# The gate/up projection of the second layer's feed-forward as seven block products, with one of four weight sums on GpSimd

## The chip, the cores and the metric

The kernel runs on one core of one Trainium2 chip. The time is the device time of one execution, in microseconds (us); the kernel before was run three times.

## The reference

Two layers of a diffusion backbone, 512 latent tokens and 256 context tokens of width 1024, all in 32-bit floating point. Each layer is a mixer (gating and attention), then a gated feed-forward; norms and modulation surround both. The second layer works on the latent tokens alone. The change is in its feed-forward:

```python
def conv_ffn(h, w_in, conv_w, conv_b, w_out):
    z = h @ w_in
    g = dwconv(z[..., :D_FF], conv_w, conv_b)
    return (jax.nn.silu(g) * z[..., D_FF:]) @ w_out
```

with D_FF = 2816, so that `w_in` is 1024 x 5632. The convolution is over three neighbouring tokens, feature by feature.

## The kernel before, in words

Every large product is made of three matmuls. A 32-bit factor is split into a high part (rounded to the matmul's format) and a low part (the rest): high x high, high x low and low x high are added in PSUM (`split_mm`, lines 293, 297 and 301). Weights come in slots of 128 x 2048 numbers (1 MB): SyncE loads slot n into `w_raw[n % 2]` (`w_load`, line 341) once VectorE has finished with slot n - 2; ScalarE rounds it (`round_hi`, line 276); VectorE subtracts (`take_lo`, line 282).

The feed-forward of the second layer (stage "ff1") has 22 slots. A slot holds 128 gate features and the 128 up features that belong to them, for all eight 128-row pieces of the depth 1024. `feature_slot` runs 48 matmuls on it (2 feature groups, 8 pieces of depth, 3 matmuls), each over 512 tokens, into two PSUM banks. The first two slots are special (`first_slots`): the tokens come out of the norm in two groups of 256, so there the matmuls are over 256 tokens, interleaved with the transposes of the second group. The other 20 slots are loops.

What follows a slot: ScalarE applies the middle tap of the convolution to the gate bank (`yb`, line 945), VectorE adds the two outer taps (line 988, twice, with a drain between), ScalarE applies SiLU (line 955), VectorE multiplies with the up bank into `A_ff_lat` (line 1001) and signals `evac`. Each engine has its own queue and takes its instructions strictly in the written order; engines wait for each other by semaphores. In `ffn_act` and `ffn_dve` these steps stand beside the rounding of the next slot, in two buffers each. The output product (stage "ffo1", `out_pe`, lines 608, 611 and 614) follows; its left factors are split by `part_hi` (line 676) and `part_lo` (line 682), the first three of them already in the last slot.

Ahead of the stage, `out_then_norm_...` ends the mixer: VectorE scales the norm (line 456), TensorE transposes (line 519), VectorE and ScalarE scale and shift into six small buffers `pre_tmp`, ScalarE rounds, VectorE and GpSimd (line 487) each make half of the low parts in `HT`.

## Time and profile before

| | us |
|---|---|
| median of 3 runs | 1748.36 |
| lowest and highest run | 1747.74, 1748.41 |
| span of the profiled execution, first to last instruction | 1744.6 |
| run median less that span (what lies around it) | 3.8 |
| TensorE busy | 1699.8 |
| VectorE busy | 1102.7 |
| ScalarE busy | 683.5 |
| GpSimd busy | 195.1 |

The profile is of one execution. The page gives the span alone; the time of the runs lies 3.8 us above it. A matmul's time in the profile is longer than the distance to the next one, since matmuls overlap: what a row of matmuls costs is read from the distance between starts.

### The profile page before, as it was taken

How to read it: one execution, taken by the hardware profiler on the slowest of the kernel's cores; microseconds unless marked ns; L12 is line 12 of the kernel's file. 1: busy time of each engine (PE TensorE's matmuls, PEld its weight loads, DVE VectorE, ACT ScalarE, POOL GpSimd, SP SyncE). 2: the span in 40 equal slices, each digit the busy share in tenths (PEclk: the TensorE clock that was granted, in tenths of full speed). 3: DMA queues.
4: the chain of work that ended last, by engine and by line, in shares of the span. 5: the costliest groups of instructions: out<-in, count | busy, mean ns of one | idle time of the engine just before them, and what ended most of it. 6: DMA issues, size and time to landing. Idle time of an engine off the chain costs nothing.

```text
span 1744.6 us, 23609 instructions
## 1 busy us (share of the span) xinstructions
PE 1699.8 (97%) x9234; PEld 1454.8 (83%) x9234; DVE 1102.7 (63%) x1745; ACT 683.5 (39%) x1127; POOL 195.1 (11%) x201
## 2 busy tenths in 40 slices
PE   6999999999999999999999999999999999999998
PEld 4788899787988888888888898879887888888777
DVE  5676777767676766644344678978875644444454
ACT  4343266544422221223344444454455422223442
POOL 1078500002100000000000210111210200000000
PEclk9999999999999999999999999999999999999999
DMA  8633000131334345441312122200012222222321
GB/s 343 215 124 116 17 22 1 75 143 49 133 128 162 138 152 193 169 134 55 114 50 95 40 102 80 97 1 1 33 42 86 95 73 96 97 97 97 131 98 71
DMA packets 40769, 173.08 MB, mean 99 GB/s; under 512 B 12640, under 2 KB 13152, under 8 KB 26208
## 3 DMA queue, kind: packets, MB, share of 16 engines
q1 hardware_dynamic: 31984, 166.75, 26.5%
q10 hardware_dynamic: 8688, 4.99, 1.0%
q8 instruction: 66, 1.08, 0.3%
q14 instruction: 31, 0.25, 0.1%
HBM read 169.60 MB, written 2.13 MB: 98 GB/s over the span
## 4 chain that ended last, share of the span: by engine, by line
PE 87%; DVE 4%; ACT 3%; DVEq 2%; issue 1%; DMA 1%; POOL 1%; ACTq 0%; SPq 0%; another core or an unknown queue 0%
PE PS L297 14%; PE PS L293 14%; PE PS L301 14%; PE PS L608 8%; PE PS L614 8%; PE PS L611 8%; PE PS L1120 4%; PE PS L325 3%; PE PS L328 3%; PE PS L329 3%; PE PS L1105 2%; DMA mod_raw<-modw 1%; DVE w_lo L282 1%; DVEq L1165 1%; ACT w_hi L276 1%
## 5 line engine op out<-in xcount | busy, mean ns | idle before, releaser
L293 PE MATMUL PS<-HT,w_hi 128*128 128x512 f32 (+1 forms) x1248 | 375.6, 347 | 0.0
L297 PE MATMUL PS<-HT,w_hi 128*128 128x512 f32 (+1 forms) x1248 | 375.5, 347 | 0.0
L301 PE MATMUL PS<-HT,w_lo 128*128 128x512 f32 (+1 forms) x1248 | 372.1, 344 | 0.0
L282 DVE TENSOR_TENSOR w_lo<-w_raw,w_hi 128x2048 fp32r<-128x2048 f32 x100 | 231.4, 2314 | 168.4 <-ACT w_hi L276 162.3
L608 PE MATMUL PS<-w_hi,a_ring 128*128 128x512 f32 x670 | 262.8, 392 | 2.9 <-DVE w_lo L282 0.9
L611 PE MATMUL PS<-w_lo,a_ring 128*128 128x512 f32 x670 | 260.9, 389 | 0.0
L276 ACT ACTIVATE w_hi<-w_raw 128x2048 fp32r<-128x2048 f32 x99 | 188.9, 1908 | 160.9 <-PE PS L608 103.7
L301 PEld LDWEIGHTS PS<-HT,w_lo 128*128 128x128 f32 x1248 | 211.7, 189 | 31.9
L293 PEld LDWEIGHTS PS<-HT,w_hi 128*128 128x128 f32 x1248 | 209.5, 188 | 29.9
L297 PEld LDWEIGHTS PS<-HT,w_hi 128*128 128x128 f32 x1248 | 210.6, 189 | 28.5
L988 DVE SCALAR_TENSOR_TENSOR yb<-PS,cws,yb 128x511 f32<-128x511 f32 (+1 forms) x132 | 83.1, 658 | 155.4 <-ACTq L949 151.0
L945 ACT ACTIVATE yb<-PS,cws 128x512 f32<-128x512 f32 x44 | 34.3, 780 | 338.4 <-PE PS L301 338.4
L608 PEld LDWEIGHTS PS<-w_hi,a_ring 128*128 128x128 f32 x670 | 125.8, 188 | 32.7 <-DVE w_lo L282 3.0
L611 PEld LDWEIGHTS PS<-w_lo,a_ring 128*128 128x128 f32 x670 | 125.8, 188 | 25.3
L819 POOL TENSOR_TENSOR rstd<-rstd,halfneg 128x1 f32<-128x1 f32 x20 | 11.0, 550 | 1145.1 <-DVE rstd L771 1145.0
L614 PE MATMUL PS<-w_hi,a_ring 128*128 128x512 f32 x340 | 132.4, 389 | 0.0
L415 DVE SCALAR_TENSOR_TENSOR m_raw<-m_raw,c_rows 128x1024 f32<-128x1024 f32 x80 | 102.1, 1276 | 30.9 <-DMA m_raw<-modu 28.9
L325 PE MATMUL PS<-w_hi,HT 128*128 128x512 f32 (+1 forms) x272 | 103.1, 379 | 0.5 <-DVE HT L1964 0.5
L329 PE MATMUL PS<-w_hi,HT 128*128 128x512 f32 (+1 forms) x272 | 102.0, 375 | 0.0
L328 PE MATMUL PS<-w_lo,HT 128*128 128x512 f32 (+1 forms) x272 | 102.0, 375 | 0.0
L2096 DVE SCALAR_TENSOR_TENSOR cat_od<-G,ccw,cat_od 128x512 f32<-128x512 f32 x120 | 86.0, 751 | 4.3 <-issue 0.4
L1164 DVE TENSOR_REDUCE rmax<-PS 128x1 f32<-128x768 f32 (+1 forms) x72 | 66.6, 924 | 15.9 <-PE PS L1082 14.4
(321 smaller groups left out, 2660.0 us busy)
## 6 DMA issues: line engine op xcount, KB each, us to landing
w_raw<-wpack SPq DMA_DIRECT2D x102, 1024.0 KB, 4.8
m_raw<-modu SPq DMA_DIRECT2D x80, 512.0 KB, 4.3
mod_raw<-modw SPq DMA_DIRECT2D x8, 1024.0 KB, 11.7
c_rows<-c_scratch SPq DMA_DIRECT2D x6, 512.0 KB, 5.2
X<-x SPq DMA_DIRECT2D x2, 1024.0 KB, 6.5
out<-X SPq DMA_DIRECT2D x4, 512.0 KB, 2.6
X<-ctx SPq DMA_DIRECT2D x1, 1024.0 KB, 10.0
gmB<-gate_rows_evo ACTq DMA_DIRECT2D x1, 1024.0 KB, 4.5
```

What stands on the lines that cost most here:

```text
L276: nc.scalar.activation(w_hi[r][:, :], w_raw[r][:, :], ACT.Copy).then_inc(wh_ready, 1)
L282: nc.vector.tensor_tensor(w_lo[r][:, :], w_raw[r][:, :], w_hi[r][:, :].bitcast(F32), ALU.subtract).then_inc(wl_ready, 1)
L293: mm = nc.tensor.matmul(o, wh, xh, start=start, stop=False)
L297: mm = nc.tensor.matmul(o, wh, xl, start=False, stop=False)
L301: last = nc.tensor.matmul(o, wl, xh, start=False, stop=stop)
L325: mm = nc.tensor.matmul(o, xh, w_hi[r][:, wc], start=k == 0, stop=False)
L328: nc.tensor.matmul(o, xh, w_lo[r][:, wc], start=False, stop=False)
L329: return nc.tensor.matmul(o, xl, w_hi[r][:, wc], start=False, stop=k == KD - 1)
L415: nc.vector.scalar_tensor_tensor(out=raw if g == sets - 1 else ps2(m_banks(c)[0], D), in0=raw, scalar=1.0, in1=c_rows[c_phase(c)][g][:, :] ...
L608: mm = nc.tensor.matmul(o, ah, w_hi[n % 2][:, wc], start=k == 0, stop=False)
L611: mm = nc.tensor.matmul(o, ah, w_lo[n % 2][:, wc], start=False, stop=False)
L614: return nc.tensor.matmul(o, al, w_hi[n % 2][:, wc], start=False, stop=k == kt - 1)
```

## The change

In slots 2 to 21 of "ff1" the product is written as a 2 x 2 block product. The blocks are: gate or up features; even or odd pieces of the depth; first or second 128 tokens of each group of 256. The eight block products become seven. Each is 12 matmuls over 256 tokens, so a slot has 84 in place of 48 of 512. Four of the seven use sums or differences of weight blocks (`Sw`), the others plain blocks; four use differences of token blocks (`TH`, `TL`, made once). All seven weights are split into `FH[0..6]` (ScalarE, `form_hi`, seven roundings of 512 numbers) and `FL[0..6]` (VectorE, `form_lo`). Three of the sums are made by VectorE (`form_sum` 0, 1, 3), one by GpSimd (`third_sum`). Products share three PSUM banks x, w, y; several are added onto a bank whose content is first copied out by ScalarE (`seven_keep`: p1, p5, u2, u3). VectorE joins the parts: `gate` makes `Gf`, from which the convolution now reads; `up_sum` adds the two kept pieces in `zp`; `evacuate` multiplies in two halves. The loops are written out. The norm ahead keeps its values in `h_pre3` and no longer in the six buffers; GpSimd and VectorE make the token differences there. Some semaphores are shared under other names. The order of the loads on SyncE is as before; a load's release is now the seventh `form_lo` of the slot two before.

```diff
+        h_pre3 = [at("h_pre3_0", R_X + 16 * KIB, [P, KD, 256]), at("h_pre3_1", R_A + 8 * KIB, [P, KD, 256])]
+        TH, TL = ([at(f"{name}{i}", off + part * 4 * KIB, [P, KD // 2, 2, P], F32R) for i, off in
+                   enumerate((R_HT + 32 * KIB, R_HT + 40 * KIB, R_A + 44 * KIB, R_A + 52 * KIB))]
+                  for part, name in enumerate(("TH", "TL")))
+        FH, FL = ([at(f"{name}{i}", off + (i % 4) * 2 * KIB + (1 - i // 4) * 8 * KIB, [P, KD // 2, P], F32R) for i in range(7)]
+                  for off, name in ((R_WH, "FH"), (R_WL, "FL")))
+        Sw = [at(f"Sw{i}", R_MOD + 2 * i * KIB, [P, KD // 2, P]) for i in range(4)]
+        pu = at("pu", R_A + 60 * KIB, [P, 2, 256])
+        zp = at("zp", R_A + 62 * KIB, [P, 2, 256])
+        up = at("up", R_A + 64 * KIB, [P, LAT])
+        Gf = at("Gf", R_GM + 6 * KIB, [P, LAT])
 
...
+        SUM_OF = {1: 0, 2: 1, 4: 2, 5: 3}
+        RAW_OF = {0: (0, 0), 3: (1, 0), 6: (1, 1)}
+        RIGHT_OF = {0: (0, 0), 3: (1, 0), 5: (1, 1)}
+        TURNED_OF = {1: 0, 2: 1, 4: 2, 6: 3}
+        BANK_OF = ("x", "y", "x", "w", "x", "y", "x")
+        ONTO = (2, 4, 5, 6)
+        TURNED = (0, 2, 1, 3)
...
+        def formed(s, i):
+            return 6 * s + ((0, 2, 3, 1, 4, 5)[i] if s == 0 else i) + 1
...
+        def product_done(eng, s, i):
+            if i == 6:
+                eng.wait_ge(w_used, F11 + 2 + s + 1)
+            else:
+                eng.wait_ge(S("sv", "prod"), 6 * s + i + 1)
+        def form_sum(dve, s, j):
+            n = F11 + 2 + s
+            a11, a12, a21, a22 = (raw_part(n, k, m) for m in range(2) for k in range(2))
+            if j == 0:
+                raw_landed(dve, n)
+            if j == 3:
+                dve.wait_ge(S("sv", "sum"), 3 * s + 2)
+            x, y, op = {0: (a21, a22, ALU.add), 1: (Sw[0][:, :, :], a11, ALU.subtract),
+                        3: (a12, Sw[1][:, :, :], ALU.subtract)}[j]
+            nc.vector.tensor_tensor(Sw[j][:, :, :], x, y, op).then_inc(S("sv", "sum"), 1)
+        def third_sum(pool, s):
+            n = F11 + 2 + s
+            raw_landed(pool, n)
+            if s:
+                pool.wait_ge(S("sv", "lo"), formed(s - 1, 4))
+            nc.gpsimd.tensor_tensor(Sw[2][:, :, :], raw_part(n, 0, 0), raw_part(n, 0, 1), ALU.subtract)\
+                .then_inc(S("sv", "tsum0"), 1)
+        def form_hi(act, s, i):
+            if i == 4:
+                act.wait_ge(S("sv", "tsum0"), len(TURNED) + s + 1)
+            elif i in SUM_OF:
+                act.wait_ge(S("sv", "sum"), 3 * s + {1: 1, 2: 2, 5: 3}[i])
+            else:
+                raw_landed(act, F11 + 2 + s)
+            if s:
+                product_done(act, s - 1, i)
+            else:
+                act.wait_ge(w_used, F11 - 1 if i < 4 else F11 + 2)
+            nc.scalar.activation(FH[i][:, :, :], form_source(s, i), ACT.Copy)\
+                .then_inc(wh_ready if i == 6 else S("sv", "hi"), 1)
+        def form_lo(dve, s, i):
+            if i == 6:
+                dve.wait_ge(wh_ready, F11 + 2 + s + 1)
+            else:
+                dve.wait_ge(S("sv", "hi"), formed(s, i))
+            nc.vector.tensor_tensor(FL[i][:, :, :], form_source(s, i), FH[i][:, :, :].bitcast(F32), ALU.subtract)\
+                .then_inc(wl_ready if i == 6 else S("sv", "lo"), 1)
...
+        def turned_sum(eng, ops, g, t):
+            if t == 0:
+                eng.wait_ge(S("pre3", "hi"), since("pre3", "hi") + KD * (g + 1))
+                eng.wait_ge(S("pre3", "lo_even"), since("pre3", "lo_even") + KD // 2 * (g + 1))
+            if t == 1:
+                eng.wait_ge(S("pre3", "lo_odd"), since("pre3", "lo_odd") + KD // 2 * (g + 1))
+            eng.drain()
+            b11, b12, b21, b22 = (half_tokens(g, k, h) for k in range(2) for h in range(2))
+            x, y = ((b12, b11), (b22, b11), (b22, b12), (b21, b22))[t]
+            ops.tensor_tensor(turned_place(g, t), x, y, ALU.subtract).then_inc(S("sv", f"tsum{g}"), 1)
...
+        def seven_pe(pe):
+            first_slots(pe, "pre3", F11, 2)
+            for s in range(JF - 2):
+                ns = s + 2
+                for i in range(7):
+                    if i == 6:
+                        pe.wait_ge(wl_ready, F11 + ns + 1)
+                    else:
+                        pe.wait_ge(S("sv", "lo"), formed(s, i))
+                    if i == 0:
+                        pe.wait_ge(S("ff1", "evac"), since("ff1", "evac") + s + 1)
+                    if s == 0 and i in TURNED_OF:
+                        pe.wait_ge(S("sv", "tlo"), 2 * TURNED.index(TURNED_OF[i]) + 2)
+                    if i in (2, 4, 5, 6):
+                        pe.wait_ge(S("sv", "kept"), 4 * s + {2: 1, 4: 3, 5: 3, 6: 4}[i])
+                    o = PS[:, seven_bank(ns, BANK_OF[i]), 0:256].rearrange("p (g c) -> p g c", g=2)
+                    for q in range(KD // 2):
+                        if i in RIGHT_OF:
+                            k, h = RIGHT_OF[i]
+                            xh, xl = (HT[:, 0:2, part, 2 * q + k, h * P:(h + 1) * P] for part in range(2))
+                        else:
+                            t = TURNED_OF[i]
+                            xh, xl = TH[t][:, q, :, :], TL[t][:, q, :, :]
+                        onto = i in ONTO
+                        begins, ends = q == 0 and not onto, q == KD // 2 - 1
+                        nc.tensor.matmul(o, FH[i][:, q, :], xh, start=begins, stop=False, skip_group_check=onto)
+                        nc.tensor.matmul(o, FH[i][:, q, :], xl, start=False, stop=False, skip_group_check=onto)
+                        last = nc.tensor.matmul(o, FL[i][:, q, :], xh, start=False, stop=ends, skip_group_check=onto)
+                    last.then_inc(w_used if i == 6 else S("sv", "prod"), 1)
...
+        def seven_keep(act, s, which):
+            ns = s + 2
+            what, i, dst = {"p1": ("x", 0, pu[:, 0, :]), "p5": ("y", 1, zp[:, 1, :]), "u2": ("x", 2, pu[:, 1, :]),
+                            "u3": ("x", 4, zp[:, 0, :])}[which]
+            product_done(act, s, i)
+            if s and which == "p1":
+                act.wait_ge(S("sv", "gate"), s)
+            if s and which == "p5":
+                act.wait_ge(S("sv", "up"), s)
+            nc.scalar.activation(dst, PS[:, seven_bank(ns, what), 0:256], ACT.Copy).then_inc(S("sv", "kept"), 1)
...
+            for g in range(2):
+                turned_hi(act, g, 0)
+            plain(0)
+            form_hi(act, 0, 1)
+            for g in range(2):
+                turned_hi(act, g, 2)
+            silu(0)
+            form_hi(act, 0, 2)
+            for t in (1, 3):
+                for g in range(2):
+                    turned_hi(act, g, t)
+            plain(1)
+            form_hi(act, 0, 4)
+            form_hi(act, 0, 5)
+            silu(1)
+            form_hi(act, 0, 6)
+            for s in range(JF - 2):
+                ns, last = s + 2, s == JF - 3
+                def next_hi(i):
+                    if not last:
+                        form_hi(act, s + 1, i)
+                seven_keep(act, s, "p1")
+                next_hi(0)
+                seven_keep(act, s, "p5")
+                if s:
+                    silu(ns - 1)
+                next_hi(1)
+                seven_keep(act, s, "u2")
+                next_hi(2)
+                if last:
+                    act.wait_ge(S("ff1", "evac"), since("ff1", "evac") + JF - 1)
+                    part(0)
+                    part(1)
+                    product_done(act, s, 3)
+                    round_hi(act, F21)
+                next_hi(3)
+                seven_keep(act, s, "u3")
+                next_hi(4)
+                act.wait_ge(S("sv", "gate"), s + 1)
+                act.wait_ge(S("ff1", "evac"), since("ff1", "evac") + ns - 1)
+                conv_tap(ns, Gf[:, :])
+                next_hi(5)
+                next_hi(6)
+            silu(JF - 1)
+            act.wait_ge(w_used, F21)
+            part(2)
+            round_hi(act, F21 + 1)
...
+            def gate(s):
+                dve.wait_ge(S("sv", "kept"), 4 * s + 3)
+                product_done(dve, s, 5)
+                w = seven_bank(s + 2, "w")
+                nc.vector.tensor_tensor(by_half(Gf[:, :]), pairs(PS[:, w:w + 2, 0:256]), pairs(pu[:, :, :]), ALU.add)\
+                    .then_inc(S("sv", "gate"), 1)
+            def up_sum(s):
+                dve.wait_ge(S("sv", "kept"), 4 * s + 4)
+                nc.vector.tensor_tensor(up[:, 0:256], zp[:, 0, :], zp[:, 1, :], ALU.add).then_inc(S("sv", "up"), 1)
+            def evacuate(s):
+                j = s + 2
+                dve.wait_ge(S("ff1", "silu"), since("ff1", "silu") + j + 1)
+                dve.wait_ge(S("sv", "up"), s + 1)
+                product_done(dve, s, 6)
+                y, a = by_half(yb[j % 2][:, 0:LAT]), by_half(A_ff_lat[:, j, :])
+                x = PS[:, seven_bank(j, "x"), 0:256].rearrange("p (g c) -> p g c", g=2)
+                nc.vector.tensor_tensor(a[:, 0], y[:, 0], x, ALU.mult)
+                nc.vector.tensor_tensor(a[:, 1], y[:, 1], up[:, 0:256].rearrange("p (g c) -> p g c", g=2), ALU.mult)\
+                    .then_inc(S("ff1", "evac"), 1)
+            for t in TURNED:
+                turned_sum(dve, nc.vector, 1, t)
+            form_lo(dve, 0, 0)
+            form_lo(dve, 0, 3)
+            form_sum(dve, 0, 0)
+            for g in range(2):
+                turned_lo(dve, g, 0)
+            conv(0, PS[:, 0, :])
+            form_sum(dve, 0, 1)
+            form_sum(dve, 0, 3)
+            form_lo(dve, 0, 1)
+            for g in range(2):
+                turned_lo(dve, g, 2)
+            gated(0, PS[:, 1, :])
+            form_lo(dve, 0, 2)
+            for t in (1, 3):
+                for g in range(2):
+                    turned_lo(dve, g, t)
+            conv(1, PS[:, 3, :])
+            form_lo(dve, 0, 4)
+            form_lo(dve, 0, 5)
+            gated(1, PS[:, 4, :])
+            form_sum(dve, 1, 0)
+            for s in range(JF - 2):
+                ns, last = s + 2, s == JF - 3
+                def next_lo(i):
+                    if not last:
+                        form_lo(dve, s + 1, i)
+                def next_sum(j):
+                    if not last:
+                        form_sum(dve, s + 1, j)
+                form_lo(dve, s, 6)
+                if s:
+                    conv(ns - 1, Gf, lambda: next_sum(0))
+                else:
+                    dve.drain()
+                next_sum(1)
+                next_lo(0)
+                if s:
+                    up_sum(s - 1)
+                next_lo(1)
+                if s:
+                    evacuate(s - 1)
+                next_sum(3)
+                next_lo(2)
+                if last:
+                    part(0)
+                next_lo(3)
+                next_lo(4)
+                if last:
+                    take_lo(dve, F21)
+                gate(s)
+                next_lo(5)
+            conv(JF - 1, Gf)
+            part(1)
+            up_sum(JF - 3)
+            evacuate(JF - 3)
+            part(2)
+            take_lo(dve, F21 + 1)
...
+        def seven_pool(pool):
+            for t in (1, 3):
+                turned_sum(pool, nc.gpsimd, 0, t)
+            for s in range(JF - 2):
+                third_sum(pool, s)
...
                 round_hi(act, n_next + 1)
+                form_hi(act, 0, 0)
+                form_hi(act, 0, 3)
                 pre_high(act, sp, KD, 2 * KD)
...
             else:
+                for t in (0, 2):
+                    turned_sum(pool, nc.gpsimd, 0, t)
                 pre_low(pool, sp, KD, 2 * KD)
...
-            ffn_act(act, "ff1", 1, F11, LAT, lambda q: part_hi(act, "ffo1", q, JF, LT, A_ff_lat))
+            seven_act(act, lambda q: part_hi(act, "ffo1", q, JF, LT, A_ff_lat))
...
-            ffn_pe(pe, "ff1", F11, LAT, False, "pre3")
+            seven_pe(pe)
...
-            ffn_dve(dve, "ff1", 1, F11, LAT, A_ff_lat, False, lambda q: part_lo(dve, "ffo1", q, JF, LT, A_ff_lat))
+            seven_dve(dve, lambda q: part_lo(dve, "ffo1", q, JF, LT, A_ff_lat))
```

**VectorE, the end of one slot of the loop before and the next slot.** `w_raw` is the loaded slot, `cws` the taps, `yb` the gate branch, `PS` PSUM:

```order
L1001 TENSOR_TENSOR A_ff_lat<-yb_170,PS 128x512
L281 REGISTER_ALU
L282 TENSOR_TENSOR w_lo_56<-w_raw_52,w_hi_54 128x2048 [waits wh_ready]
L973 ISA
L973 COPY cws_89<-cw 128x4
L983 REGISTER_ALU
L988 SCALAR_TENSOR_TENSOR yb_171<-PS,cws_89,yb_171 128x511 [waits ff1_mid]
L988 SCALAR_TENSOR_TENSOR yb_171<-PS,cws_89,yb_171 128x511
```

**VectorE, from `gate` of one slot into the next slot, in the change.** L828 is `gate`, L661 `form_lo`, L629 `form_sum`, L807 and L811 the two outer taps, L833 `up_sum`, L842 and L843 `evacuate`; `ff_mid` comes from ScalarE's middle tap, `sv_hi` from its roundings, `sv_kept` from its copies:

```order
L828 TENSOR_TENSOR Gf<-PS,pu 128x2x2x128 [waits sv_prod,sv_kept]
L661 TENSOR_TENSOR FL_211<-Sw_216,FH_204 128x512 [waits sv_hi]
L661 TENSOR_TENSOR FL_212<-w_raw_52,FH_205 128x512 [waits wh_ready]
L807 SCALAR_TENSOR_TENSOR yb_165<-Gf,cw,yb_165 128x511 [waits ff_mid]
L629 TENSOR_TENSOR Sw_213<-w_raw_51 128x512 [waits landed0]
L811 SCALAR_TENSOR_TENSOR yb_165<-Gf,cw,yb_165 128x511
L629 TENSOR_TENSOR Sw_214<-Sw_213,w_raw_51 128x512
L661 TENSOR_TENSOR FL_206<-w_raw_51,FH_199 128x512 [waits sv_hi]
L833 TENSOR_TENSOR up<-zp 128x256 [waits sv_kept]
L661 TENSOR_TENSOR FL_207<-Sw_213,FH_200 128x512 [waits sv_hi]
L842 TENSOR_TENSOR A_ff_lat<-yb_165,PS 128x2x128 [waits w_used,sv_up,ff_silu]
L843 TENSOR_TENSOR A_ff_lat<-yb_165,up 128x2x128
```

The five instructions of a slot became sixteen (twelve are shown); the taps stand behind `gate` and two `form_lo`, `evacuate` behind `up_sum` and a `form_lo`.

**ScalarE, two slots before** (L276 rounds the next slot, L945 is the middle tap, L955 SiLU):

```order
L276 ACTIVATE w_hi_54<-w_raw_52 128x2048 [waits w_used,landed1]
L945 ACTIVATE yb_171<-PS,cws_89 128x512 [waits w_used,ff1_tap]
L955 ACTIVATE yb_171<-yb_171 128x512 [waits ff1_conv]
L276 ACTIVATE w_hi_53<-w_raw_51 128x2048 [waits w_used,landed0]
L945 ACTIVATE yb_170<-PS,cws_88 128x512 [waits w_used,ff1_tap]
L955 ACTIVATE yb_170<-yb_170 128x512 [waits ff1_conv]
```

**ScalarE, from the middle tap of one slot to the third copy of the next, in the change.** L743 is the middle tap, L652 `form_hi`, L738 `seven_keep`, L748 SiLU:

```order
L743 ACTIVATE yb_164<-Gf,cw 128x512 [waits ff_evac,sv_gate]
L652 ACTIVATE FH_204<-Sw_216 128x512 [waits sv_prod,sv_sum]
L652 ACTIVATE FH_205<-w_raw_51 128x512 [waits w_used,landed0]
L738 ACTIVATE pu<-PS 128x256 [waits sv_gate,sv_prod]
L652 ACTIVATE FH_199<-w_raw_52 128x512 [waits sv_prod,landed1]
L738 ACTIVATE zp<-PS 128x256 [waits sv_up,sv_prod]
L748 ACTIVATE yb_164<-yb_164 128x512 [waits ff_conv]
L652 ACTIVATE FH_200<-Sw_213 128x512 [waits sv_prod,sv_sum]
L738 ACTIVATE pu<-PS 128x256 [waits sv_prod]
L652 ACTIVATE FH_201<-Sw_214 128x512 [waits sv_prod,sv_sum]
L652 ACTIVATE FH_202<-w_raw_52 128x512 [waits sv_prod,landed1]
```

Here the second copy of the slot (`zp`) waits for `sv_up`, VectorE's `up_sum`; SiLU, the rounding of `FH_200` and the copy after it stand behind that wait.

## Rows read from the trace of the kernel before

**Rows 1.** The page, busy time of each engine (us, share of the span, instructions).
```profile
PE 1699.8 (97%) x9234; PEld 1454.8 (83%) x9234; DVE 1102.7 (63%) x1745; ACT 683.5 (39%) x1127; POOL 195.1 (11%) x201
```
**Rows 2.** Stretches: length, busy us of PE, PEld, DVE, ACT, POOL, granted clock, DMA share, GB/s.
```profile
1398.40:1615.80 217.40, 217.40 (x960) 180.06 (x960) 91.86 (x101) 65.54 (x62) 0.00 (x0) 1.00 0.26 95
...
20.00:40.00 20.00, 17.27 (x97) 10.89 (x96) 11.55 (x21) 7.90 (x9) 0.00 (x0) 0.91 1.00 394
...
1374.00:1384.00 10.00, 7.08 (x59) 6.67 (x59) 8.27 (x16) 5.58 (x9) 3.06 (x5) 1.00 0.27 102
```
**Rows 3.** Timeline of TensorE: start us, us, instruction, count [idle before it <- releaser].
```profile
1374.56 0.28 PE L297 MATMUL PS<-HT,w_next_hi 128*128 128x256 f32 x1
1374.68 0.28 PE L301 MATMUL PS<-HT,w_next_lo 128*128 128x256 f32 x1
1377.50 0.44 PE L519 MATMUL PS<-ident,xn_pre 128*128 128x128 f32 x2 [2.54 <-DVE xn_pre L456]
...
1398.23 0.40 PE L293 MATMUL PS<-HT,w_hi 128*128 128x512 f32 x1
...
1439.74 0.39 PE L293 MATMUL PS<-HT,w_hi 128*128 128x512 f32 x1
1439.96 0.39 PE L297 MATMUL PS<-HT,w_hi 128*128 128x512 f32 x1
...
1615.86 0.39 PE L608 MATMUL PS<-w_hi,a_ring 128*128 128x512 f32 x1
...
1621.76 0.50 PE L608 MATMUL PS<-w_hi,a_ring 128*128 128x512 f32 x1 [0.30 <-DVE w_lo L282]
```
**Rows 4.** Timeline of ScalarE and VectorE in a slot of the loop.
```profile
1444.42 0.63 ACT L955 ACTIVATE yb<-yb 128x512 f32<-128x512 f32 x1 [1.66 <-DVE yb L988]
1444.96 1.90 ACT L276 ACTIVATE w_hi<-w_raw 128x2048 fp32r<-128x2048 f32 x1
...
1442.81 1.57 DVE L988 SCALAR_TENSOR_TENSOR yb<-PS,cws,yb 128x511 f32<-128x511 f32 x2 [4.43 <-ACTq L949]
1446.89 2.29 DVE L282 TENSOR_TENSOR w_lo<-w_raw,w_hi 128x2048 fp32r<-128x2048 f32 x1 [1.00 <-ACT w_hi L276]
```
**Rows 5.** VectorE's groups (count | busy us, mean ns | idle before), and three instructions in a row.
```profile
L682 DVE TENSOR_TENSOR A_ff_lat_lo<-A_ff_lat,a_ring 128x512 fp32r<-128x512 f32 x22 | 13.8, 685 | 0.1
L475 DVE TENSOR_TENSOR HT<-pre_tmp_pre,HT 128x256 fp32r<-128x256 f32 x32 | 13.7, 427 | 1.3 <-ACT HT L508 0.6
...
1627.08 1.89 DVE L682 TENSOR_TENSOR a_ring<-A_ff_lat,a_ring 128x512 fp32r<-128x512 f32 x3
```
**Rows 6.** ScalarE's groups, and two of its instructions in a row.
```profile
L676 ACT ACTIVATE a_ring<-A_ff_lat 128x512 fp32r<-128x512 f32 x43 | 25.1, 620 | 22.3 <-PE PS L614 17.2 <-DVE A_ff_lat L1001 2.5 <-DVE cws L973 2.4
L1043 ACT ACTIVATE qTh<-PS 128x256 fp32r<-128x256 f32 x8 | 3.1, 384 | 1.0 <-PE PS L1030 0.7
...
1313.98 1.51 ACT L1627 ACTIVATE cat_od<-cat_od,ccln 128x512 f32<-128x512 f32 x2
```
**Rows 7.** Timeline of ScalarE and VectorE ahead of the loop.
```profile
1392.73 0.78 ACT L945 ACTIVATE yb<-PS,cws 128x512 f32<-128x512 f32 x1 [5.70 <-PE PS L301]
...
1393.57 1.57 DVE L988 SCALAR_TENSOR_TENSOR yb<-PS,cws,yb 128x511 f32<-128x511 f32 x2 [4.13 <-ACTq L949]
1395.84 0.69 DVE L1001 TENSOR_TENSOR A_ff_lat<-yb,PS 128x512 f32<-128x512 f32 x1 [0.70 <-ACT yb L955]
```
**Rows 8.** GpSimd beside VectorE: a group of GpSimd, then three instructions of the timeline.
```profile
L1403 POOL TENSOR_TENSOR sqs<-sqs,sqs 128x512 f32<-128x512 f32 x3 | 4.0, 1326 | 0.5 <-issue 0.5
...
1368.93 1.28 DVE L813 SCALAR_TENSOR_TENSOR X<-O_both_odo,rstd,X 128x1024 f32<-128x1024 f32 x1
1370.49 0.60 DVE L475 TENSOR_TENSOR HT<-pre_tmp_pre,HT 128x256 fp32r<-128x256 f32 x1 [0.29 <-ACT HT L508]
...
1369.59 1.22 POOL L487 TENSOR_TENSOR HT<-pre_tmp_pre,HT 128x256 fp32r<-128x256 f32 x1 [1.30 <-ACT HT L508]
```
**Rows 9.** The page, DMA issues: KB each, median us from issue to landing.
```profile
w_raw<-wpack SPq DMA_DIRECT2D x102, 1024.0 KB, 4.8
```

109 lines of the change are left out of this document (81 added, 28 removed).

## The prediction

> **What bounds the kernel now.** I read the page first, then the second feed-forward by stretches and in order of time. TensorE is busy for 97% of the span, the others for far less [rows 1]. In the 217.4 us of slots 2 to 21 it never pauses: 217.4 us busy, at full granted clock, VectorE 91.9, ScalarE 65.5, GpSimd nothing [rows 2]. The loop starts at 1398.23 and the output product at 1615.86, so a slot takes 217.63 / 20 = 10.88 us. That is 48 starts 0.22 to 0.23 us apart; where matmuls run over 256 tokens, starts are 0.12 apart [rows 3]. VectorE and ScalarE wait in every slot, since one short chain follows it and nothing waits for that chain at once [rows 4]. So TensorE's own work is the bound, and fewer columns would shorten the stage, as long as the work fed to TensorE keeps up.
>
> **What TensorE gains.** Seven products of 12 matmuls at 0.12 us are 84 x 0.12 = 10.08 us a slot, 0.80 less than now, or 16 us over 20 slots. I take 0.12 for any weights, since only the shape sets it in those rows.
>
> **What a slot now asks of VectorE and ScalarE.** Prices first. A VectorE `tensor_tensor` of 512 numbers lasts 0.685 us, but three in a row last 1.89, so the next starts after 0.60; one of 256 lasts 0.43 and, with the same 0.09 taken off, frees the engine after 0.34, with 0.35 used here [rows 5]. Two taps with a drain between last 1.57, one alone 0.75; so a drain adds 0.07, and a tap frees the engine after 0.66 [rows 4, 5]. ScalarE: 512 numbers 0.62, free after 0.54 (SiLU start to the next start); 256 from PSUM 0.384, free after 0.30; 512 from SBUF with scale and bias 0.80, free after 0.71 (1.51 less 0.80) [rows 4, 6]. From the end on one engine to the start on another pass 0.03 to 0.04: rounding ends at 1446.86 and VectorE starts at 1446.89, the taps end at 1444.38 and SiLU starts at 1444.42 [rows 4]. I take 0.035.
>
> Busy time alone fits: VectorE 11 x 0.60 + 1.50 + 0.35 + 0.70 = 9.15 us, ScalarE 7 x 0.54 + 4 x 0.30 + 0.71 + 0.54 = 6.2, both under 10.08. But each queue is in written order and the two wait for each other twice in a slot. Starting at `gate` and ending at the next slot's `gate`, the ring is:
> - `gate` 0.685 + 0.035 to ScalarE: 0.72.
> - Middle tap 0.71, then the rounding of piece 5 0.62 + 0.035: 1.365. VectorE has only `form_lo` 5 next, so it stands still.
> - `form_lo` 5 and 6: 1.20.
> - First outer tap 0.66, the sum put between (0.685 and 0.07 for the drain, 0.76), second tap 0.66: 2.08.
> - `form_sum` 1 and `form_lo` 0: 1.20.
> - `up_sum` 0.43 + 0.035: 0.465. ScalarE has waited for it with the copy "p5", because `zp` holds the last slot's part.
> - That copy 0.30, SiLU 0.54, the rounding of piece 1 0.62 + 0.035: 1.495. VectorE stands still again, at `form_lo` 1.
> - `form_lo` 1 0.60, `evacuate` 2 x 0.35, `form_sum` 3 and `form_lo` 2, 3, 4 2.40: 3.70.
>
> Together 12.22 us. Nothing in it depends on TensorE: that needs the copy "u2" before product 4, which comes 0.3 us behind the rounding of piece 1, and then it pauses about 2.1 us a slot. So **the ring, not TensorE, sets the slot**: 12.22 against 10.88, 1.34 us worse.
>
> **The ends.** Ahead of the loop TensorE now waits for `evac` of slot 0. VectorE starts the taps of slot 0 at about 1393.6 as now [rows 7]; then come 1.50, five `tensor_tensor` (3.0) and the multiplication (0.69), end 1398.8: 0.6 after the loop's old start. In the first seven-product slot, ScalarE's first copy stands behind SiLU of slot 1, which waits for VectorE: six `tensor_tensor` after 1398.1 (3.6), taps 1.57, then SiLU, a rounding and the copy, end about 1404.8; product 2 wants it at 1398.85 + 2.88 = 1401.7. That slot ends at about 1412.1, 13.9 after 1398.23, so 3.0 worse than now. Then 18 slots at +1.34 are 24.1, and the last, where the next slot's steps fall away and one whole weight slot is split, takes some 11.3 (+0.4). The output product starts 27.5 later. There its third part waits for `gate`, tap (0.72 + 0.84), taps 1.57, SiLU 0.54, part 0.54, rounding 1.9 and subtraction 2.29, about 8.5 us after 1643.3, thus at 1651.8, against 1621.76 now, a shift of 30.0 [rows 3]. Later parts keep it.
>
> **Edits that I cost at nothing.** The load of a slot is issued after `form_lo` 6, lands 4.8 us later [rows 9], and is first read in the following slot, some 8 us later; a later release would eat that first. In the norm the six small buffers fall away, and their waits with them; TensorE there waits for the scaled norm, which stays [rows 3]. The two roundings in front (1.1 us) fit in the 2.8 us in which ScalarE waits for scaled values. GpSimd's two token sums there (1.27 us each [rows 8]) may keep VectorE from the subtraction that TensorE waits for behind the pause at 1377.50: 0 to 1.0 us, taken as 0.
>
> **GpSimd's weight sum.** A sum of 512 numbers takes GpSimd 1.27 us, or up to 1.43 (the mean of three is 1.33) [rows 8]. It starts when `form_lo` 4 ends, beside `gate` (which reads PSUM) and VectorE's wait of 1.4 us, and its result is wanted most of a slot later. So it costs nothing, and saves VectorE 0.60 on the ring, already left out above. What it could cost: GpSimd and VectorE hinder each other. A GpSimd instruction of 256 numbers that usually takes 0.74 took 1.22 beside one of VectorE with two SBUF inputs, and the VectorE instruction behind it took 0.60 in place of 0.43 [rows 8]. The bound is 0 to 1.3 us a slot; I take 0. The Trainium skill (SBUF — State Buffer, Who interferes with whom) says that a GpSimd instruction reading SBUF and a VectorE one with two SBUF inputs exclude each other altogether, whoever comes first. By that rule, and if the sum fell on the ring, each slot would lose up to GpSimd's whole 1.3 us; the rows show the exclusion and smaller losses. That is a rival below.
>
> The Trainium skill (VectorE: DVE Perf Modes, The DRAIN you can't avoid) also says that the next VectorE operation doesn't start until the pipe is empty, though one that isn't held may start earlier. If all eleven on the ring went at 0.685 the slot would be 13.2 us; the rows above show 0.60 in a row.
>
> **Sum.** 1748.4 + 30.0 = 1778.4 us (span 1744.6 + 30 = 1774.6; what lies around it, 3.8, stays).
>
> **The rivals.**
> - **The products win** (faster). If VectorE and ScalarE stay a slot ahead, TensorE sets the pace from slot 3 on: 13.9 + 19 x 10.08 = 205.4 against 217.6, and with the 2.4 at the output product 1738.5 us. For it: both are under 10.08 us busy. Against: the ring closes within a slot and gets no shorter by starting early. It decides once the ring is under 10.88; the whole wait at `form_lo` 1 and some of that at `form_lo` 5 would have to go. 0.04.
> - **Only the first of the two stops counts**: were the copy "p5" not in ScalarE's way, VectorE's ring would be 12.22 less 1.96 (`up_sum`, copy, SiLU, rounding) plus 0.35, 10.6 us, and the time about 1748.5, no change. Against: in the order above ScalarE's rows stand as counted. 0.06.
> - **GpSimd or the drain lies on the ring too**: 1.0 to 1.3 us more a slot, 1797 to 1803. Speaks for it: rows 8; against: the sum's place beside `gate`. 0.07.
> - **The change doesn't do what it says**: TensorE's work doesn't shrink, because the pauses cost it its clock. A granted clock of 0.91 stands early in the program, between 20 and 40 us, where TensorE had long idled; around the single pause of 2.54 us it is 1.00 [rows 2, 3]. At the lower of the two levels (1.2 in place of 2.4 GHz) a matmul of 256 would last about 0.23, as one of 512 does now, 84 x 0.23 = 19.3 us a slot: 1748 + 170. 0.03.
>
> **How the numbers follow.** My forecast has 0.80. Its own spread: with no time between engines and 0.57 for 0.60 the ring is 11.8 and the time 1770; with 0.64, and copies that free ScalarE only after 0.42, it is 12.8 and 1790. The range 1766 to 1792 holds it nearly whole and leaves the rivals out. Around 0.2% (3.5 us) is what can be told from no change: slower 0.90, same 0.05, faster 0.05.
>
> **What would show it.** In the profile after, TensorE's first matmuls of a slot lie 12.2 us apart, with a pause of about 2 us before product 4 put down to ScalarE's copy; `form_lo` 1 and `form_lo` 5 wait 1.3 to 1.6 us each for ScalarE's rounding; "p5" waits for `up_sum`; GpSimd's sum takes 1.3 us. Slots 10.1 apart without pauses would prove me wrong, as would `form_lo` 1 that never waits.

## The result, and the profile after

Four runs of the changed kernel have a median of 1805.74 us (1803.64 to 1807.28), four of the kernel before beside them 1748.05 (1746.98 to 1748.41). The ratio is 1.0331, 95% interval 1.0317 to 1.0346. The forecast was 1778.4, range 1766 to 1792: the sign was right, the slow-down twice what was said. The span grew from 1744.6 to 1804.6 us, by 60.0; the sum had 30.0.

The page after, busy time of each engine, against [rows 1]:

```profile
PE 1718.2 (95%) x9954; PEld 1507.1 (84%) x9954; DVE 1210.3 (67%) x1975; ACT 751.9 (42%) x1335; POOL 230.3 (13%) x225
```

TensorE's busy time rose from 1699.8 to 1718.2 us, though each slot has 84 short matmuls where it had 48 long ones and should need less. The stretches say why (columns as in [rows 2]): the granted clock is no longer 1.00.

```profile
1430.00:1460.00 30.00, 26.25 (x193) 25.90 (x192) 20.26 (x35) 15.22 (x31) 2.59 (x3) 0.89 0.21 70
1460.00:1660.00 200.00, 171.86 (x1221) 169.25 (x1220) 138.00 (x236) 92.62 (x190) 18.13 (x14) 0.87 0.23 80
1660.00:1700.00 40.00, 36.90 (x208) 31.58 (x208) 24.14 (x30) 19.61 (x27) 0.00 (x0) 1.00 0.36 122
```

TensorE's timeline in one slot, where [rows 3] had starts 0.12 apart throughout:

```profile
1451.72 0.36 PE L723 MATMUL PS<-TH,FH 128*128 128x256 f32 x1 [1.88 <-ACT pu L738]
...
1452.16 0.41 PE L723 MATMUL PS<-TH,FH 128*128 128x256 f32 x1
1452.38 0.41 PE L724 MATMUL PS<-TL,FH 128*128 128x256 f32 x1
...
1455.15 0.41 PE L725 MATMUL PS<-HT,FL 128*128 128x256 f32 x1
1455.37 0.36 PE L723 MATMUL PS<-HT,FH 128*128 128x256 f32 x1
1455.56 0.28 PE L724 MATMUL PS<-HT,FH 128*128 128x256 f32 x1
```

Ahead of product 4 TensorE pauses 1.88 us for ScalarE's copy "u2" (`pu`, L738), as foreseen. Then, from the fourth matmul on, 15 lie (1455.37 - 1452.16) / 15 = 0.214 us apart, and after that 0.12 again. Three short stretches of this slot, before, in and behind that piece:

```profile
1442.80:1451.60 8.80, 7.05 (x59) 6.84 (x58) 5.76 (x10) 4.48 (x10) 0.90 (x1) 1.00 0.36 121
1452.10:1455.30 3.20, 3.20 (x17) 3.20 (x17) 2.44 (x6) 1.42 (x3) 0.00 (x0) 0.50 0.00 0
1455.40:1463.00 7.60, 7.60 (x65) 7.60 (x65) 5.63 (x9) 2.76 (x5) 1.29 (x1) 0.99 0.26 77
```

For 3.2 us the granted clock is 0.50, the lower of the two levels (1.2 GHz), and 1.00 up to the pause. The Trainium skill (TensorE: Matmul & The Clock Gate, Part 1: The HAM clock gate) says that at that level matmuls start their columns divided by 1.2 GHz apart. For 256 columns that makes an estimate of 0.213 us, and the trace agrees with its 0.214. From the start of product 4 to that of product 6, at 1456.16, pass 4.44 us, where 24 starts at 0.12 would be 2.88: 1.5 us too many.

VectorE and ScalarE in that slot:

```profile
1442.76 0.69 DVE L828 TENSOR_TENSOR Gf<-PS,pu 128x512 f32<-128x512 f32 x1 [0.50 <-PE PS L725]
1444.85 0.69 DVE L661 TENSOR_TENSOR FL<-Sw,FH 128x512 fp32r<-128x512 f32 x1 [1.41 <-ACT FH L652]
...
1449.38 0.42 DVE L833 TENSOR_TENSOR up<-zp 128x256 f32<-128x256 f32 x1
1451.34 0.69 DVE L661 TENSOR_TENSOR FL<-Sw,FH 128x512 fp32r<-128x512 f32 x1 [1.54 <-ACT FH L652]
...
1455.26 0.69 DVE L661 TENSOR_TENSOR FL<-Sw,FH 128x512 fp32r<-128x512 f32 x1 [0.76 <-ACT FH L652]
1456.43 0.69 DVE L828 TENSOR_TENSOR Gf<-PS,pu 128x512 f32<-128x512 f32 x1 [0.48 <-PE PS L725]
```

```profile
1449.89 0.38 ACT L738 ACTIVATE zp<-PS 128x256 f32<-128x256 f32 x1 [3.42 <-PE PS L725]
1450.17 0.62 ACT L748 ACTIVATE yb<-yb 128x512 f32<-128x512 f32 x1
1450.69 0.62 ACT L652 ACTIVATE FH<-Sw 128x512 fp32r<-128x512 f32 x1
1451.20 0.37 ACT L738 ACTIVATE pu<-PS 128x256 f32<-128x256 f32 x1
```

`form_lo` 5 waits 1.41 us and `form_lo` 1 waits 1.54, as foreseen (1.3 to 1.6). The copy "p5" (`zp`) is put down to TensorE, but that was long done: it starts 0.09 us after `up_sum` (L833) ends. What is new are the waits of 0.76 us at `form_lo` 4 and 0.48 at `gate`, for product 5. The slot is 1456.43 - 1442.76 = 13.67 us, and the 18 from gate to gate are 246.5 us in all, 13.70 each.

### The profile page after: what moved, and what is told of

Read it like the earlier page. It is cut to its first block and busy times, and to the rows that moved or that the text cites. A ratio compares the mean times of both kernels' runs of the same rounds, so it can differ in the third digit from the quotient of the medians.

```text
span 1804.6 us, 25614 instructions
## 1 busy us (share of the span) xinstructions
PE 1718.2 (95%) x9954; PEld 1507.1 (84%) x9954; DVE 1210.3 (67%) x1975; ACT 751.9 (42%) x1335; POOL 230.3 (13%) x225
## 5 line engine op out<-in xcount | busy, mean ns | idle before, releaser
L297 DVE TENSOR_TENSOR w_lo<-w_raw,w_hi 128x2048 fp32r<-128x2048 f32 x80 | 186.1, 2326 | 149.3 <-ACT w_hi L291 145.0
L308 PE MATMUL PS<-HT,w_hi 128*128 128x256 f32 (+1 forms) x928 | 251.1, 332 | 0.0
L312 PE MATMUL PS<-HT,w_hi 128*128 128x256 f32 (+1 forms) x928 | 251.0, 332 | 0.0
L316 PE MATMUL PS<-HT,w_lo 128*128 128x256 f32 (+1 forms) x928 | 247.6, 328 | 0.0
L291 ACT ACTIVATE w_hi<-w_raw 128x2048 fp32r<-128x2048 f32 x80 | 152.8, 1910 | 163.1 <-PE PS L958 106.1
L316 PEld LDWEIGHTS PS<-HT,w_lo 128*128 128x128 f32 x928 | 151.6, 189 | 19.3
L312 PEld LDWEIGHTS PS<-HT,w_hi 128*128 128x128 f32 x928 | 150.5, 189 | 16.3
L308 PEld LDWEIGHTS PS<-HT,w_hi 128*128 128x128 f32 x928 | 149.4, 188 | 17.4
L723 PE MATMUL PS<-TH,FH 128*128 128x256 f32 x320 | 100.0, 313 | 37.4 <-ACT pu L738 37.0
L1299 ACT ACTIVATE yb<-PS,cws 128x512 f32<-128x512 f32 x22 | 17.2, 780 | 214.1 <-PE PS L316 214.1
L723 PEld LDWEIGHTS PS<-TH,FH 128*128 128x128 f32 x320 | 68.7, 215 | 40.9 <-issue 37.9
L661 DVE TENSOR_TENSOR FL<-Sw,FH 128x512 fp32r<-128x512 f32 x80 | 55.1, 689 | 71.1 <-ACT FH L652 71.1
```

Of the source, the lines that this page charges most:

```text
L291: nc.scalar.activation(w_hi[r][:, :], w_raw[r][:, :], ACT.Copy).then_inc(wh_ready, 1)
L297: nc.vector.tensor_tensor(w_lo[r][:, :], w_raw[r][:, :], w_hi[r][:, :].bitcast(F32), ALU.subtract).then_inc(wl_ready, 1)
L308: mm = nc.tensor.matmul(o, wh, xh, start=start, stop=False)
L312: mm = nc.tensor.matmul(o, wh, xl, start=False, stop=False)
L316: last = nc.tensor.matmul(o, wl, xh, start=False, stop=stop)
L723: nc.tensor.matmul(o, FH[i][:, q, :], xh, start=begins, stop=False, skip_group_check=onto)
```

## The experiments

All times are medians, with the ratio to the kernel before run beside them on the same chip. There are two theories. **A**: the two-queue ring is 12.22 us as counted, and the other 1.45 us come from TensorE's clock, since the way through "u2", product 4 and product 5 becomes longer than VectorE's own. **B**: something on VectorE or GpSimd is dearer than counted (the exclusion, the drains), and TensorE's slow matmuls are hidden.

### 16 matmuls in the pause (`e1_fill16`)

```diff
+                    if s and i == 4:
+                        for r in range(16):
+                            nc.tensor.matmul(PS[:, 7, 0:256].rearrange("p (g c) -> p g c", g=2), TH[0][:, r % 4, 0, :],
+                                             TH[0][:, r % 4, :, :], start=True, stop=True)
```

> The change, with 16 matmuls over 256 tokens put into TensorE's pause ahead of product 4 of slots 3 to 21 (they multiply one token difference with itself into a PSUM bank that nobody reads). Theory A (the pause costs TensorE its clock, and the slow products 4 and 5 lengthen the ring by 1.45 us): 16 x 0.12 = 1.9 us fill the pause, granted clock 1.00, slot 12.2 in place of 13.67 us, time 1805.7 - 19 x 1.45 = 1778. Theory B (the slow matmuls have another cause, say the kind of operand, or the ring takes 13.7 us without them): slot 13.6 or more, time 1805 or above.

1781.69 us (1779.89 to 1783.48, two runs), ratio 1.0203 (1.0182 to 1.0223). More work for TensorE makes the kernel some 23 us faster. The stretch, and VectorE's two waits of a slot:

```profile
1420.00:1500.00 80.00, 79.45 (x654) 78.41 (x652) 59.70 (x105) 40.92 (x84) 7.79 (x6) 1.00 0.27 93
```

```profile
1481.16 0.69 DVE L661 TENSOR_TENSOR FL<-Sw,FH 128x512 fp32r<-128x512 f32 x1 [1.41 <-ACT FH L652]
...
1487.65 0.69 DVE L661 TENSOR_TENSOR FL<-Sw,FH 128x512 fp32r<-128x512 f32 x1 [1.55 <-ACT FH L652]
```

The clock is 1.00, the waits at `form_lo` 4 and `gate` are gone, and the middle taps start at 1479.79 and 1492.05: the slot is 12.26 us. By its parts it is what was counted: 2.09 us from `gate` to `form_lo` 5 (counted 2.09), 6.49 on to `form_lo` 1 (6.44), 3.68 on to the next `gate` (3.70). Theory A holds, and the forecast's ring with it.

### 8 matmuls in the pause (`e1b_fill8`)

The same edit with `range(8)`.

> The changed kernel with 8 extra matmuls (into a bank nobody reads) in TensorE's pause ahead of product 4, half of those of e1_fill16. They fill 8 x 0.12 = 0.96 of the 1.88 us pause. Theory 'the clock falls only on the long pause': a pause of about 0.9 us is left, the granted clock stays at 1.00, slot 12.25 us, about 1780 us like e1_fill16. Rival 'any pause above half a microsecond brings the clock down in proportion': clock between 0.90 and 0.98, slot about 13.0, about 1793 us. That each pause costs the same whatever its length: about 1805.

1780.65 us (1779.35 to 1781.36), ratio 1.0192 (1.0177 to 1.0207). TensorE pauses for 0.99 us in each slot and keeps its clock:

```profile
1459.68 0.36 PE L727 MATMUL PS<-TH,FH 128*128 128x256 f32 x1 [0.99 <-ACT pu L742]
1471.94 0.36 PE L727 MATMUL PS<-TH,FH 128*128 128x256 f32 x1 [0.99 <-ACT pu L742]
```

```profile
1430.00:1600.00 170.00, 156.07 (x1276) 153.63 (x1275) 127.38 (x223) 88.30 (x180) 18.15 (x14) 1.00 0.26 88
```

So a pause of 0.99 us in every slot costs nothing here, where one of 1.88 us does. (The next run shows that the length alone doesn't settle it.)

### The third weight sum on VectorE (`e3_third_dve`)

In the body of `third_sum`, called from VectorE's queue behind `form_sum` 3, the waits counted to match:

```diff
-            nc.gpsimd.tensor_tensor(Sw[2][:, :, :], raw_part(n, 0, 0), raw_part(n, 0, 1), ALU.subtract)\
-                .then_inc(S("sv", "tsum0"), 1)
+            nc.vector.tensor_tensor(Sw[2][:, :, :], raw_part(n, 0, 0), raw_part(n, 0, 1), ALU.subtract)\
+                .then_inc(S("sv", "sum"), 1)
```

> The change, with the fourth weight sum made by VectorE behind form_sum 3 and no longer by GpSimd. Theory A: VectorE waits 0.74 + 0.48 us per slot at form_lo 4 and gate for ScalarE and TensorE, so 0.60 us more work is hidden; the time stays within 2 us of 1805.7, perhaps 1 us less since GpSimd no longer holds VectorE up at the start. Theory B (VectorE's work is on the path everywhere, as my forecast had it): 19 x 0.60 = 11 us more, 1817.

1802.75 us (1801.19 to 1804.66), ratio 1.0322 (1.0305 to 1.0339), which can't be told from the change's own (1.0317 to 1.0346): what VectorE spends more fits in the 1.24 us that it waits behind `form_lo` 1. GpSimd's sum, which is the change's last part, earns nothing in this order. The run's trace also shows two kinds of slot. Three of TensorE's restarts, and 3.5 us behind each of them:

```profile
1451.07 0.36 PE L723 MATMUL PS<-TH,FH 128*128 128x256 f32 x1 [2.55 <-ACT pu L738]
1463.93 0.55 PE L723 MATMUL PS<-TH,FH 128*128 128x256 f32 x1 [2.56 <-ACT pu L738]
1477.53 0.36 PE L723 MATMUL PS<-TH,FH 128*128 128x256 f32 x1 [1.88 <-ACT pu L738]
```

```profile
1451.00:1454.50 3.50, 3.43 (x29) 3.46 (x30) 3.50 (x8) 1.98 (x4) 0.00 (x0) 1.00 0.00 0
1464.00:1467.50 3.50, 3.50 (x18) 3.50 (x19) 3.31 (x7) 1.46 (x4) 0.00 (x0) 0.55 0.02 5
1477.60:1481.10 3.50, 3.50 (x30) 3.50 (x31) 3.50 (x8) 1.84 (x4) 0.00 (x0) 1.00 0.03 7
```

Where the clock stays, the slot is 1463.93 - 1451.07 = 12.86 us, the ring of 12.22 and the added 0.60. Where it falls, it is 13.60 (1477.53 - 1463.93), and 13.65 to 13.68 in the slots from 1491 on, where the clock falls each time. So the length of the pause alone doesn't decide: one of 2.55 us passes and the next costs the clock, and the one of 1.88 us at 1477.53, as long as those of the changed kernel, passes too. What does decide stays open.

### `up_sum` early (`e2_up_early`)

```diff
-                if s:
-                    up_sum(s - 1)
                 next_lo(1)
...
                 gate(s)
+                if s:
+                    dve.wait_ge(S("ff1", "evac"), since("ff1", "evac") + s + 2)
+                up_sum(s)
                 next_lo(5)
```

> The change, with up_sum moved from behind form_lo 0 of the next slot to right behind gate, where VectorE stands still for ScalarE. Theory A (the ring is set by the stop of ScalarE at copy p5, which waits for up_sum): the ring loses 1.96 us, 10.3 us are left, TensorE pauses 0.2 us or less and keeps its clock, slot 10.3, time 1805.7 - 19 x 3.4 = 1742. If a short pause costs the clock too: slot 11.7, time 1769. Theory B (VectorE's amount of work or GpSimd's hold on it sets the slot): the same work, so 1800 or above.

1747.07 us (1743.55 to 1749.29), ratio 1.0003 (0.9993 to 1.0013). One line's place was worth some 58 us: "p5" no longer waits, the ring opens, the pause and, in the loop, the slow matmuls are gone. The slot is 10.40 us, 0.1 above the 10.3 expected and 0.3 above TensorE's own 10.08. In it:

```profile
1485.59 0.68 DVE L828 TENSOR_TENSOR Gf<-PS,pu 128x512 f32<-128x512 f32 x1
1486.19 1.20 DVE L833 TENSOR_TENSOR up<-zp 128x256 f32<-128x256 f32 x1
1487.68 0.69 DVE L661 TENSOR_TENSOR FL<-Sw,FH 128x512 fp32r<-128x512 f32 x1 [0.28 <-ACT FH L652]
```

```profile
1485.82 1.30 POOL L637 TENSOR_TENSOR Sw<-w_raw 128x512 f32<-128x512 f32 x1 [9.11 <-DVE FL L661]
```

GpSimd works from 1485.82 to 1487.12. `gate`, which reads PSUM, isn't touched; `up_sum`, with both inputs in SBUF, lasts 1.20 us in place of 0.42 and ends at 1487.39, just behind it. So GpSimd held it up, by 0.8 us a slot. How much of that reaches the length of the slot this run doesn't show. The Trainium skill (SBUF — State Buffer, Who interferes with whom) calls this an exclusive lock held for the whole instruction; the trace agrees.

### `up_sum` early and `form_lo` 4 behind `gate` (`e4_up_lo4`)

```diff
-                next_lo(4)
                 if last:
                     take_lo(dve, F21)
                 gate(s)
+                next_lo(4)
```

> As the run with up_sum behind gate, and form_lo 4 behind gate too, also in VectorE's idle time. Theory A: the ring is 9.7 us, under TensorE's 84 x 0.12 = 10.08, so TensorE sets the slot, with no pause and full clock; time 1805.7 - 19 x 3.59 = 1737.5. Theory B (something else holds it above 10.08, or a pause stays and takes the clock): 1742 or above.

1754.78 us (1751.29 to 1756.75), ratio 1.0048 (1.0031 to 1.0065): a miss. GpSimd's sum, released by `form_lo` 4, now runs beside `form_lo` 5, and holds it up (0.69 us before):

```profile
1481.51 1.23 DVE L661 TENSOR_TENSOR FL<-Sw,FH 128x512 fp32r<-128x512 f32 x1 [0.47 <-ACT FH L652]
```

The slot is 1490.26 - 1479.41 = 10.85 us, closed by taps, SiLU, "u2" and product 4 and 5. TensorE pauses 0.55 us in each slot, and the clock is 1.00 from 1430 to 1600.

### Token sums on VectorE, then the order of slot 2 (`e5_start`, `e6_order`)

First all eight token sums (`turned_sum`) on VectorE. GpSimd's four fall away, and its first weight sum waits for the four of the first half of the tokens. Then SiLU and multiply of slot 1 moved behind "u2" and `form_lo` 1 of slot 2.

```diff
             for t in TURNED:
-                turned_sum(dve, nc.vector, 1, t)
+                for g in range(2):
+                    turned_sum(dve, nc.vector, g, t)
```

```diff
-            silu(1)
             form_hi(act, 0, 6)
...
                 seven_keep(act, s, "u2")
+                if not s:
+                    silu(1)
```

> e2_up_early with all eight token sums on VectorE (GpSimd makes none; its first weight sum waits until they are done). Theory 'GpSimd beside VectorE holds VectorE up': the w_lo subtraction returns from 3.26 to 2.29 us, the eight sums take about 8 x 0.62 = 5.0 us where four took 6.3 beside GpSimd, the loop of slots starts 2.3 us earlier, 1744.8 us. Rival 'the sums are slow by themselves (their drains)': eight take 12 us, the first product comes 4 us later, 1751.

> e5_start, and the SiLU of slot 1 moves behind the copy of u2 of slot 2 on ScalarE, and its multiply behind form_lo 1 on VectorE, so that the copies of slot 2 no longer wait for the convolution of slot 1. Theory: the 2.84 us wait of TensorE ahead of product 4 of slot 2 goes, and nothing else waits in its place: e5_start less 2.5, about 1742. Rival 'VectorE alone sets the first slots, since its queue is full': no change against e5_start.

1747.39 us (1744.72 to 1748.77), ratio 1.0000 (0.9991 to 1.0009), and 1745.64 us (1743.11 to 1748.68), ratio 0.9991 (0.9982 to 0.9999). The first expected 1744.8 and lies between its theory and its rival. VectorE ahead of the loop, with `up_sum` early alone and then in the second of the two:

```profile
1375.59 3.26 DVE L297 TENSOR_TENSOR w_lo<-w_raw,w_hi 128x2048 fp32r<-128x2048 f32 x1
...
1384.55 6.30 DVE L682 TENSOR_TENSOR h_pre<-h_pre 128x512 f32<-128x512 f32 x4 [0.17 <-DVE HT L494]
```

```profile
1376.64 2.29 DVE L297 TENSOR_TENSOR w_lo<-w_raw,w_hi 128x2048 fp32r<-128x2048 f32 x1
...
1384.49 7.88 DVE L682 TENSOR_TENSOR h_pre<-h_pre 128x512 f32<-128x512 f32 x8
```

GpSimd beside it did cost the `w_lo` subtraction 0.97 us. The eight sums last 7.88 us. Taken one by one, the six between the first and the last take 0.69 us each and start 0.78 apart; the first and the last take longer, and each has a GpSimd instruction beside it:

```profile
1384.49 1.27 DVE L682 TENSOR_TENSOR h_pre<-h_pre 128x512 f32<-128x512 f32 x1
1389.77 0.69 DVE L682 TENSOR_TENSOR h_pre<-h_pre 128x512 f32<-128x512 f32 x1
1390.56 1.82 DVE L682 TENSOR_TENSOR h_pre<-h_pre 128x512 f32<-128x512 f32 x1
...
1384.47 0.73 POOL L506 TENSOR_TENSOR HT<-h_pre,HT 128x256 fp32r<-128x256 f32 x1 [0.63 <-ACT HT L513]
1390.54 1.29 POOL L637 TENSOR_TENSOR Sw<-w_raw 128x512 f32<-128x512 f32 x1 [5.33 <-DVE h_pre L682]
```

So the drain ahead of a sum costs 0.18 us (starts 0.78 apart, 0.60 without one), and 0.58 + 1.13 = 1.7 us are again what GpSimd holds up, the larger part through its first weight sum, which starts ahead of the last token sum. On VectorE the eight take 1.6 us longer than the four did, of which the subtraction gives back 0.97. The first product starts 24.09 us behind the restart after the norm's pause (1400.75 - 1376.66), with `up_sum` early alone 23.61 (1399.22 - 1375.61). TensorE, there earlier, waits 3.20 us ahead of it where it waited 1.75.

The second edit brings less than foreseen. The 2.84 us stood ahead of product 2, for the copy "p1", and not ahead of product 4 as the expectation says. They are gone, but 2.32 us now stand ahead of product 4: "u2" stands behind a rounding that waits for a sum that comes late on VectorE and is held up by GpSimd there (1.76 us in place of 0.69).

### Half of `evacuate` beside GpSimd (`e7_half`)

```diff
                 gate(s)
+                if s and not last:
+                    evacuate(s - 1, (0,))
```

and at the old place the other half alone, which announces nothing.

> e6_order, and the half of evacuate that reads PSUM is put between gate and up_sum, so that up_sum starts later in GpSimd's sum. Theory 'only VectorE operations with both operands in SBUF are held by GpSimd': the PSUM half takes its 0.41 us beside GpSimd, up_sum is held 0.35 us less, slot from 10.41 to about 10.1 (TensorE's own 84 x 0.12 = 10.08), 18 x 0.3 = 5.5 us less than e6_order, about 1737. Rival 'every VectorE operation is held': the half is held as up_sum was, slot stays 10.4, same time as e6_order.

1745.67 us (1743.53 to 1746.17), ratio 0.9989 (0.9980 to 0.9998). As expected the half that reads PSUM takes 0.41 us beside GpSimd and `up_sum` 0.76 in place of 1.20, but the slot only falls from 10.39 to 10.35:

```profile
1539.46 0.69 DVE L829 TENSOR_TENSOR Gf<-PS,pu 128x512 f32<-128x512 f32 x1
1540.06 0.41 DVE L845 TENSOR_TENSOR A_ff_lat<-yb,PS 128x256 f32<-128x256 f32 x1
1540.50 0.76 DVE L834 TENSOR_TENSOR up<-zp 128x256 f32<-128x256 f32 x1
1541.55 0.69 DVE L661 TENSOR_TENSOR FL<-Sw,FH 128x512 fp32r<-128x512 f32 x1 [0.28 <-ACT FH L652]
```

So 0.44 us less of being held up shorten the slot by 0.05. `form_lo` 4 now waits 0.19 us for ScalarE's rounding, which it did not before. The ring through taps, SiLU, "u2" and product 4 is still there, and is the bound to attack next.

### The ring taken apart (`e8_ring`)

```diff
-                if s:
-                    silu(ns - 1)
                 next_hi(1)
                 seven_keep(act, s, "u2")
-                if not s:
-                    silu(1)
+                silu(ns - 1)
...
+                next_hi(5)
                 act.wait_ge(S("sv", "gate"), s + 1)
                 act.wait_ge(S("ff1", "evac"), since("ff1", "evac") + ns - 1)
                 conv_tap(ns, Gf[:, :])
-                next_hi(5)
```

On VectorE `form_lo` 6 goes behind the two outer taps.

> e7_half, with ScalarE's queue reordered: form_hi 1 and the copy of u2 ahead of the SiLU, form_hi 5 ahead of the middle tap; on VectorE the two outer taps ahead of form_lo 6. Nothing is left on the way from the gate to product 4 that waits for the convolution. Theory: TensorE alone sets the slot, 84 x 0.12 = 10.08 to 10.15 us against 10.35, 18 x 0.23 = 4 us less, about 1741.5. Rival 'VectorE's queue is full, 10.35 is its own work': same as e7_half, 1745.7.

1742.95 us (1740.62 to 1744.26), ratio 0.9977 (0.9968 to 0.9986). TensorE works without a pause, at full clock, and the slot is 1547.47 - 1537.30 = 10.17 us:

```profile
1500.00:1560.00 60.00, 60.00 (x498) 59.78 (x497) 56.24 (x96) 39.91 (x77) 7.77 (x6) 1.00 0.30 106
```

Here the products win, as the first rival had it.

### The head of the stage (`e9_drain`, `e10_first`)

Three drains in place of eight; then, with that, slot 0's multiply and "u2" of slot 2 each one place earlier.

```diff
-            eng.drain()
+            if g == 0 and t in (0, 1, 3):
+                eng.drain()
```

```diff
+            gated(0, PS[:, 1, :])
             for g in range(2):
                 turned_lo(dve, g, 2)
-            gated(0, PS[:, 1, :])
...
-                next_hi(1)
+                if s:
+                    next_hi(1)
                 seven_keep(act, s, "u2")
+                if not s:
+                    next_hi(1)
```

> e8_ring, and the token sums of the first half (g) and second half drain VectorE three times in all instead of eight times. Theory: the eight sums took 7.9 us where 8 x 0.61 = 4.9 is their work; the rest are drains ahead of the loop. They take about 5.3 us, the loop of slots starts 2.6 us earlier, and TensorE's wait ahead of the first product falls from 3.2 to about 0.6 us: e8_ring less 2.6, about 1739. Rival 'the wait ahead of the first product is set by something else behind the sums': same as e8_ring.

> e9_drain with two changes ahead of and in slot 2 alone: VectorE multiplies slot 0's output ahead of two low parts of token sums, ScalarE copies u2 of slot 2 ahead of form_hi 1. Theory 'TensorE's waits of 2.26 us ahead of the first product and 2.33 us ahead of product 4 of slot 2 are queue order': each falls by about 1.2 us, e9_drain less 2 to 2.4, about 1739.4. Rival 'VectorE is full from 1386 to 1412, so what is made earlier makes something else late': the waits move, same time as e9_drain (1741.6).

1741.59 us (1740.11 to 1743.37), ratio 0.9968 (0.9957 to 0.9979). The sums fell from 7.89 to 5.85 us: five drains less at 0.18 are 0.9, and the other 1.1 is the last sum, which GpSimd no longer holds up. But GpSimd's sum then held the next two subtractions up (2.39 us where they took 1.28), so the wait ahead of the first product only fell from 3.20 to 2.26 us. The expectation had taken all 3 us above 8 x 0.61 for drains:

```profile
1386.71 5.85 DVE L683 TENSOR_TENSOR h_pre<-h_pre 128x512 f32<-128x512 f32 x8
1392.47 2.39 DVE L661 TENSOR_TENSOR FL<-w_raw,FH 128x512 fp32r<-128x512 f32 x2
```

1740.73 us (1739.34 to 1742.30), ratio 0.9960 (0.9947 to 0.9974): of the 2.26 us ahead of the first product 1.06 are left, while product 4's 2.33 are gone and 2.10 now stand ahead of product 6, for "u3". VectorE's queue up to 1412 is full, and the rival was half right: the time fell by 0.9 us, and the intervals of the two runs overlap. It is the lowest median of all, 0.4% below the kernel before.

### The same without GpSimd (`e11_third_dve2`)

`third_sum` on VectorE again, in the last kernel.

> e10_first with the third weight sum on VectorE, so that GpSimd does nothing in this stage behind the norm. VectorE's queue of a slot is about 10.17 - 0.50 idle - 0.35 held + 0.60 = 9.9 us, still under TensorE's 10.08 to 10.17. Theory 'GpSimd's sum earns nothing, since it holds VectorE up nearly as long as the sum would take there': slot 10.1 to 10.2, within 2 us of e10_first. Rival 'GpSimd's sum is worth its 0.6 us a slot': 18 x 0.5 = 9 us slower.

1741.14 us (1739.05 to 1742.31), ratio 0.9961 (0.9947 to 0.9974), the same; the slot is 10.17 us. From 1430 to 1600, with GpSimd's sum and without:

```profile
1430.00:1600.00 170.00, 170.00 (x1407) 169.36 (x1406) 159.98 (x269) 112.06 (x216) 20.69 (x16) 1.00 0.30 106
```

```profile
1430.00:1600.00 170.00, 170.00 (x1406) 169.33 (x1405) 165.50 (x286) 112.83 (x218) 0.00 (x0) 1.00 0.30 106
```

16 sums at 0.60 are 9.6 us, but VectorE's busy time differs by 5.5 only. The rest is what GpSimd holds it up for, which counts as busy too: `up_sum` takes 0.76 us in place of 0.42 beside GpSimd's sum. TensorE is busy without a break in both, so the 5.5 us are worth nothing there.

## Why the prediction was right and wrong

**Right: the ring and what closes it.** 12.22 us were counted and 12.26 measured once the clock was kept, and its three parts agree within 0.05, so the sum isn't right by chance. Its two stops stood where they were put, at 1.41 and 1.54 us within the 1.3 to 1.6 foreseen, and the pause ahead of product 4 was 1.88 against about 2. That the copy "p5" is what closes it was shown by moving `up_sum`.

**Wrong: "Nothing in it depends on TensorE".** This is the step that failed. It took 0.12 us for every matmul, "since only the shape sets it in those rows", and read TensorE's pause of about 2.1 us as time to spare. In the trace 15 of the starts behind that pause lie 0.214 us apart, at a granted clock of 0.50. There is a second ring, through TensorE: from `gate` to the end of the copy "u2" pass 8.81 us, to the restart of TensorE 0.15, and through products 4 and 5 to the next `gate` 4.71, together 13.67. At full clock it would be 13.67 - 1.5 = 12.2, as long as the ring that was counted, so it had nothing to spare: the 1.5 us of slow matmuls went into the slot nearly whole. So 1.45 us a slot were missing, 18 x 1.45 = 26 of the 30 us that the sum was short.

**Wrong: how the rival on the clock was priced.** It allowed full clock or the lower level for every matmul (19.3 us a slot, 1918 us), with a chance of 0.03. The case between, the lower level for a fifth of the matmuls right after a pause, wasn't there. With the other rival, GpSimd or the drain on the ring, 1797 to 1803 us stood nearest to what came, but not by its cause: with GpSimd out of the loop the time stayed. The argument against the clock was a single pause of 2.54 us with 1.00 around it [rows 2, 3]. That was one execution. The same pause of the norm stands in all fourteen profiles (2.52 to 2.56 us): the clock stays at 1.00 behind it in nine, those of before and after among them, and falls to 0.50 around its end or within 1.5 us of it in five (`e1_fill16`, `e1b_fill8`, `e3_third_dve`, `e5_start`, `e11_third_dve2`). The 3.2 us behind its end at 1376.44 in `e1b_fill8`:

```profile
1376.80:1380.00 3.20, 3.13 (x16) 2.84 (x15) 3.20 (x2) 0.62 (x2) 3.04 (x2) 0.50 0.00 0
```

So the rows could not say that such a pause is free.

**Wrong by less: the head of the stage**, foreseen as +3.0 us. By the steps the loop started 2.9 us late (0.6 foreseen), and by `gate` of the first such slot the loss was 5.7: the output product starts at 1673.99, 57.7 later than before (the whole execution lies 0.40 later from the pause at 1377.90 on), less 18 x 2.81 and less 1.35 for the last slot, of which 0.4 was foreseen. Of it 0.97 are GpSimd's token sums, costed at 0 within 0 to 1.0: the `w_lo` subtraction took 3.26 us and TensorE waited 1.35 instead of 0.38. Four VectorE sums took 6.3 us beside GpSimd, against 4 x 0.78 = 3.1 us with their drains alone. The first had been bounded by 1.0 and taken as 0; for the second the start of VectorE's taps was taken "as now", about 1393.6, and it was 1396.06. The clock fell in this first slot too: 0.50 from 1407.8 to 1411.1, behind a pause of 2.84 us, and `form_lo` 4 there waited 0.96 us for a rounding behind the copy "u3", which came late behind the slow products 2 and 3.

**Right: GpSimd's weight sum at nothing**, in this order of queues. In the loop it ran beside `gate` and VectorE's wait and held nothing up. But the 0.60 that it was said to save is a saving only where the clock stays: there a slot is 12.86 us with the sum on VectorE and 12.26 without. In the changed kernel VectorE waits 1.24 us more than was counted, and the sum would fit in. Where VectorE had no wait to give, the sum held it up by 0.34 to 0.8 us a slot.

**Right: the output product.** At its third part, which starts at 1682.32, the shift is 60.2 us: 2.5 more, and 2.5 were foreseen. The four differences, 26, 2.7, 1.0 and 0, are the 30 us.

## What to carry to other kernels

If a change makes TensorE pause once in every turn of a loop, cost the way back through it at its lower clock too, and don't take one profile in which a pause was free as proof; a second ring that is as long as the first at full clock is the longer one then. Read a queue for the one instruction that waits for another engine's small result: one sum's place was worth some 58 us here, and the seven products themselves, in the best order found, 7. Hand work to GpSimd only where VectorE waits or reads PSUM: elsewhere it held VectorE up here by 0.34 to 0.8 us for the 0.60 that it took off.

## What had not been expected

- The clock's fall is short and regular: half clock for some 3.2 us, from 0.1 to 0.4 us behind the end of a pause of 1.88 us, in slot after slot, and none after pauses of 0.99 and 0.55 us. Yet in `e3_third_dve` pauses of 2.55 and of 1.88 us passed without one, and ahead of the stage one of 2.5 us did in nine profiles of fourteen. What decides it these runs don't show.
- Eight matmuls whose result nobody reads (0.96 us a slot) buy some 24 us.
- A drain ahead of a sum of 512 numbers moves its start from 0.60 to 0.78 us behind the one before. A GpSimd instruction beside such a sum costs more: 0.58 and 1.13 us in the two cases above.
